# The last stage of an encoder-and-experts kernel: a buffer for every tile, the expert sum on TensorE, and two small outputs stored as rows

## What is computed

```python
# hier_moe: each row t has two experts with weights wts[t, 0:2]
out = out + comb[:, e:e + 1] * (hid @ w_expert_down[e])      # two rows of the sum per token are non-zero
x = x + gt2 * hier_moe(h)                                    # gated residual
y = rmsnorm(x, normf_g) * (1 + scf) + shf                    # final norm, scale and shift: outputs 0 and 1
# outputs 2 and 5: the last projected RWKV row of prompt and sample, 1664 numbers each
```

## Time and profile before

| | us |
|---|---|
| median of 3 runs (lowest, highest) | 1783.12 (1774.79, 1783.71) |
| the profiled execution | 1775.52 |
| its span, first to last instruction | 1773.8 |
| its first instruction of the last block | 1656.95 |

### The profile page before, as it was taken

One profiled execution on the slowest core, in us unless ns is written; L12 is line 12 of the kernel. 1 busy time (PEld: TensorE's weight loads), 2 busy tenths in 40 slices (PEclk: granted clock), 3 DMA queues, 4 the chain that ended last, 5 costly groups with the idle time before them and its releaser, 6 DMA issues. The chain is left out here.

```text
span 1773.8 us, 29923 instructions
## 1 busy us (share of the span) xinstructions
PE 1503.5 (85%) x12585; PEld 1096.1 (62%) x12585; DVE 547.6 (31%) x1006; ACT 384.8 (22%) x774; POOL 184.4 (10%) x281
## 2 busy tenths in 40 slices
PE   5899999999939999999999984699999999995100
PEld 3566665666628778776877652678878788683000
DVE  4254464302115545454545324110000000000066
ACT  5332223112113323332332220011111111100022
POOL 0011111100022001110111000100000000000031
PEclk9899999999969999999999966699999999997655
DMA  7345654422163321332132005997777877948563
GB/s 297 112 142 192 224 210 162 150 74 74 50 216 115 96 62 38 96 97 61 38 96 67 1 30 201 398 342 260 284 287 257 309 262 261 321 160 299 83 203 128
DMA packets 184095, 299.54 MB, mean 169 GB/s; under 512 B 22519, under 2 KB 94491, under 8 KB 183965
## 3 DMA queue, kind: packets, MB, share of 16 engines
q1 hardware_dynamic: 166860, 240.96, 39.7%
q0 software_dynamic: 12928, 42.79, 6.9%
q10 hardware_dynamic: 4176, 13.90, 2.0%
HBM read 241.96 MB, written 55.64 MB: 168 GB/s over the span
## 5 line engine op out<-in xcount | busy, mean ns | idle before, releaser
L2048 PE MATMUL banks<-moe_xT,moe_wg 128*128 128x160 f32 x1024 | 146.0, 301 | 0.8 <-ACT moe_xT L2168 0.8
L2048 PEld LDWEIGHTS banks<-moe_xT,moe_wg 128*128 128x128 f32 x1024 | 140.3, 190 | 7.6 <-issue 6.6
L2048 PE MATMUL banks<-moe_xT,moe_wu 128*128 128x160 f32 x1024 | 144.3, 299 | 0.0
L2048 PEld LDWEIGHTS banks<-moe_xT,moe_wu 128*128 128x128 f32 x1024 | 140.8, 190 | 0.0
L1215 PE MATMUL banks<-mixer_w_out,mixer_yT 128*128 128x512 f32 (+1 forms) x288 | 127.5, 601 | 4.5 <-DVE mixer_yT L1661 3.7
L598 PE MATMUL banks<-xT,w_v 128*128 128x352 f32 (+1 forms) x384 | 118.7, 469 | 0.0
L598 PE MATMUL banks<-xT,w_r 128*128 128x352 f32 (+1 forms) x384 | 118.6, 469 | 0.0
L598 PE MATMUL banks<-xT,w_k 128*128 128x352 f32 (+1 forms) x384 | 118.3, 468 | 0.0
L1471 POOL TENSOR_TENSOR mixer_LTm<-mixer_LT,level 128x256 f32<-128x256 f32 (+1 forms) x90 | 72.1, 825 | 407.3 <-ACT mixer_LTo L1527 282.3
L2089 PE MATMUL banks<-moe_wd,moe_hid 128*128 128x512 f32 x256 | 112.5, 592 | 0.0
L598 PEld LDWEIGHTS banks<-xT,w_v 128*128 128x128 f32 x384 | 72.6, 190 | 45.2 <-issue 2.2
(11 more groups left out here) (431 smaller groups left out, 2042.5 us busy)
## 6 DMA issues: line engine op xcount, KB each, us to landing
moe_wg<-w_expert_gate SPq DMA_DIRECT2D x20, 2048.0 KB, 9.2
moe_wu<-w_expert_up SPq DMA_DIRECT2D x20, 2048.0 KB, 11.8
moe_wd<-w_expert_down SPq DMA_DIRECT2D x20, 2048.0 KB, 10.0
w_mod<-w_ada SPq DMA_DIRECT2D x8, 2048.0 KB
mixer_feats<-feature_major SPq DMA_DIRECT2D x16, 768.0 KB, 8.4
wada<-w_ada SPq DMA_DIRECT2D x4, 2048.0 KB, 19.9
w_mod<-w_ada_final SPq DMA_DIRECT2D x4, 2048.0 KB
mixer_feats<-feature_major SPq DMA_DIRECT2D x8, 1024.0 KB, 5.8
```

What stands on the lines that cost most here:

```text
L2048: mm = pe.matmul(bank[:, i * S_STATIC:(i + 1) * S_STATIC], wt[:, u, q, (t0 + i) * P:(t0 + i + 1) * P], xT[:, e % 2, q, :], start=q == 0, s ...
```

## The change

- All 9 tiles have their own `y1`, `y2` and `x`; `x2` is written over `x`, the output over `y1`. The waits for a free buffer go. `idx` goes too: the gathers take their row numbers from `c["slots"]`. GpSimd issues all 18 gathers one behind the other without a wait; SyncE loads the first three `x` tiles at once and tile n when the gathers of tile n - 3 have landed.
- ScalarE makes, once, two diagonal matrices per tile (`diag`), the identity times each token's weight. TensorE multiplies `diag` by `y1` and `y2` and sums both products in PSUM, 4 matmuls of 128x128 by 512 columns per tile, into one of four pairs of banks. `first_share` and L2520 go; the gate product reads PSUM.
- TensorE turns the two small outputs to 13 rows of 128 numbers, ScalarE copies them to SBUF, and SyncE stores 512 B pieces, behind all its `x` loads.
- The squares go into `y2`. ScalarE issues the store of tile n - 1 after the exponential of tile n. VectorE's order of heads and tails is the same.

```diff
             experts_block(nc, a, d, c, psum, final_rows)
-            combine_block(nc, a, o, d, c, final_rows)
+            combine_block(nc, a, o, d, c, final_rows, banks)
...
-        y1, y2, x, x2, out = [sb(n, [P, 2, D]) for n in ("y1", "y2", "x", "x2", "out")]
-        idx = sb("idx", [P, 2, 2], I32)
-        st = sb("st", [P, 2, 2])
+        y1, y2, x = [sb(n, [P, NT, D]) for n in ("y1", "y2", "x")]
+        diag = sb("diag", [P, NT, 2, P])
+        st = sb("st", [P, NT, 2])
         eps = sb("eps", [P, 1])
-        slots, share = c["slots"], c["share"]
+        shifts_T = sb("shifts_T", [13, 2, P])
+        slots, share, ident = c["slots"], c["share"], c["ident"]
         GATE, SCALE, SHIFT = 0, 1, 2
         yp = o[0].rearrange("a t d -> (a t) d")
...
+        TILES = [(n, P if n < NP else DEC) for n in range(NT)]
+        def pair(n):
+            return banks[:, 1024 * (n % 4):1024 * (n % 4) + 1024]
...
         @block.sync
         def _(sp):
+            for n, m in TILES:
+                if n > 2:
+                    sp.wait_ge(sg(f"y{n - 3}_loaded"), 32)
+                sp.dma_start(x[0:m, n, :], d["x1"][n * P:n * P + m, :]).then_inc(sg(f"x{n}_loaded"), 16)
+            sp.wait_ge(sg("shifts_read"), 1)
             for r, i in ((0, 2), (1, 5)):
-                with nc.allow_non_contiguous_dma("a row of 13 x 128 from its columns"):
-                    sp.dma_start(o[i].rearrange("a b (n p) -> p (a b n)", p=P), c["shifts"][:, :, r]).then_inc(sg("shifts_out"), 16)
-            def step(n, u, m, n0, n1):
-                before = reg(sp, n - 1)
-                w(sp, "x2_made", before)
-                sp.dma_start(x[0:m, u, :], d["x1"][bass.ds(n * P, m), :]).then_inc(sg(f"x{u}_loaded"), 16)
-            tiles(sp, step)
+                sp.dma_start(o[i].rearrange("a b (n p) -> (a b n) p", p=P), shifts_T[:, r, :]).then_inc(sg("shifts_out"), 16)
             sp.wait_ge(sg("shifts_out"), 32)
         @block.gpsimd
         def _(pool):
             nc.gpsimd.memset(eps[:, :], RMS_EPS).then_inc(sg("eps_made"), 1)
-            def step(n, u, m, n0, n1):
-                before = reg(pool, n - 1)
-                w(pool, "x2_made", before)
-                nc.gpsimd.tensor_copy(idx[:, u, :], slots[:, bass.ds(n, 1), :].rearrange("p a b -> p (a b)")).then_inc(sg("idx_made"), 1)
+            for n, m in TILES:
                 for i, y in enumerate((y1, y2)):
-                    pool.wait_ge(sg("eps_made"), 1)
-                    pool.wait_ge(sg("idx_made"), n1)
-                    pool.indirect_dma_start(out=y[0:m, u, :], out_offset=None, in_=d["y"],
-                                            in_offset=bass.IndirectOffsetOnAxis(ap=idx[0:m, u, i:i + 1], axis=0)).then_inc(sg(f"y{u}_loaded"), 16)
-            tiles(pool, step)
+                    pool.indirect_dma_start(out=y[0:m, n, :], out_offset=None, in_=d["y"],
+                                            in_offset=bass.IndirectOffsetOnAxis(ap=slots[0:m, n, i:i + 1], axis=0)).then_inc(sg(f"y{n}_loaded"), 16)
+        @block.tensor
+        def _(pe):
+            for r in range(2):
+                mm = pe.transpose(banks[0:13, 7 * 512 + r * P:7 * 512 + (r + 1) * P], c["shifts"][:, :, r], ident[:, :])
+            mm.then_inc(sg("shifts_turned"), 1)
+            for n, m in TILES:
+                pe.wait_ge(sg("diag_made"), 2 * n + 2)
+                pe.wait_ge(sg(f"y{n}_loaded"), 32)
+                w(pe, "y_gated", n - 3)
+                if n == 3:
+                    pe.wait_ge(sg("shifts_read"), 1)
+                for h in range(2):
+                    for i, y in enumerate((y1, y2)):
+                        mm = pe.matmul(pair(n)[0:m, 512 * h:512 * h + 512], diag[0:m, n, i, 0:m], y[0:m, n, 512 * h:512 * h + 512],
+                                       start=i == 0, stop=i == 1)
+                mm.then_inc(sg("y_summed"), 1)
         @block.scalar
         def _(act):
             nc.scalar.preload_act_table_set("natural_log_exp_and_others")
+            act.wait_ge(sg("shifts_turned"), 1)
+            nc.scalar.copy(shifts_T[:, :, :], banks[0:13, 7 * 512:7 * 512 + 2 * P].rearrange("p (r c) -> p r c", r=2)).then_inc(sg("shifts_read"), 1)
+            for n, m in TILES:
+                for i in range(2):
+                    nc.scalar.activation(diag[:, n, i, :], ident[:, :], ACT.Copy, scale=share[:, n, i:i + 1]).then_inc(sg("diag_made"), 1)
             act.wait_ge(sg("eps_made"), 1)
-            def first_share(n, u, m):
-                act.wait_ge(sg(f"y{u}_loaded"), 16 * (n + 2 - u))
-                nc.scalar.activation(y1[0:m, u, :], y1[0:m, u, :], ACT.Copy, scale=share[0:m, n, 0:1]).then_inc(sg("y1_shared"), 1)
-            def step(n, u, m, n0, n1):
-                before = reg(act, n - 1)
-                if n == 0:
-                    first_share(0, 0, P)
-                w(act, "out_scaled", before)
-                w(act, f"out{u}_stored", 8 * (n - u))
-                w(act, "x2_made", n1)
-                nc.scalar.activation(out[0:m, u, :], x2[0:m, u, :], ACT.Square, accum_out=st[0:m, u, 0:1]).then_inc(sg("squared"), 1)
-                w(act, "squared", n1)
-                nc.scalar.activation(st[0:m, u, 1:2], st[0:m, u, 0:1], ACT.Ln, scale=1.0 / D, bias=eps[0:m, :]).then_inc(sg("log_made"), 1)
-                w(act, "log_made", n1)
-                nc.scalar.activation(st[0:m, u, 1:2], st[0:m, u, 1:2], ACT.Exp, scale=-0.5).then_inc(sg("rstd_made"), 1)
-                if n < NP:
-                    first_share(n + 1, 1 - u, DEC if n + 1 == NP else P)
-                act.wait_ge(sg("out_made"), n1)
-                dst = yp[bass.ds(n * P, m), :] if m == P else ys
-                act.dma_start(dst, out[0:m, u, :]).then_inc(sg(f"out{u}_stored"), 16)
-            tiles(act, step)
-            act.wait_ge(sg("out0_stored"), 80)
-            act.wait_ge(sg("out1_stored"), 64)
+            for n, m in TILES:
+                act.wait_ge(sg("x2_made"), n + 1)
+                nc.scalar.activation(y2[0:m, n, :], x[0:m, n, :], ACT.Square, accum_out=st[0:m, n, 0:1]).then_inc(sg("squared"), 1)
+                act.wait_ge(sg("squared"), n + 1)
+                nc.scalar.activation(st[0:m, n, 1:2], st[0:m, n, 0:1], ACT.Ln, scale=1.0 / D, bias=eps[0:m, :]).then_inc(sg("log_made"), 1)
+                act.wait_ge(sg("log_made"), n + 1)
+                nc.scalar.activation(st[0:m, n, 1:2], st[0:m, n, 1:2], ACT.Exp, scale=-0.5).then_inc(sg("rstd_made"), 1)
+                if n:
+                    act.wait_ge(sg("out_made"), n)
+                    act.dma_start(yp[(n - 1) * P:n * P, :], y1[:, n - 1, :]).then_inc(sg("out_stored"), 16)
+            act.wait_ge(sg("out_made"), NT)
+            act.dma_start(ys, y1[0:DEC, NP, :]).then_inc(sg("out_stored"), 16)
+            act.wait_ge(sg("out_stored"), 16 * NT)
...
-            def head(n, u, m, n0, n1):
+            def head(n, m):
                 r = 0 if m == P else 1
-                dve.wait_ge(sg(f"y{u}_loaded"), 16 * (n + 2 - u))
-                dve.wait_ge(sg("y1_shared"), n1)
-                V.scalar_tensor_tensor(y1[0:m, u, :], y2[0:m, u, :], share[0:m, n, 1:2], y1[0:m, u, :], ALU.mult, ALU.add).then_inc(sg("y_summed"), 1)
-                dve.wait_ge(sg("y_summed"), n1)
-                V.tensor_tensor(y1[0:m, u, :], y1[0:m, u, :], rows[0:m, r, GATE, :], ALU.mult).then_inc(sg("y_gated"), 1)
-                dve.wait_ge(sg(f"x{u}_loaded"), 8 * (n + 2 - u))
-                dve.wait_ge(sg("y_gated"), n1)
-                V.tensor_tensor(x2[0:m, u, :], x[0:m, u, :], y1[0:m, u, :], ALU.add).then_inc(sg("x2_made"), 1)
-            def tail(n, u, m, n0, n1):
+                dve.wait_ge(sg("y_summed"), n + 1)
+                V.tensor_tensor(y1[0:m, n, :], pair(n)[0:m, :], rows[0:m, r, GATE, :], ALU.mult).then_inc(sg("y_gated"), 1)
+                dve.wait_ge(sg(f"x{n}_loaded"), 16)
+                dve.wait_ge(sg("y_gated"), n + 1)
+                V.tensor_tensor(x[0:m, n, :], x[0:m, n, :], y1[0:m, n, :], ALU.add).then_inc(sg("x2_made"), 1)
+            def tail(n, m):
                 r = 0 if m == P else 1
-                dve.wait_ge(sg("rstd_made"), n1)
-                w(dve, f"out{u}_stored", 8 * (n - u))
-                V.scalar_tensor_tensor(out[0:m, u, :], x2[0:m, u, :], st[0:m, u, 1:2], rows[0:m, r, SCALE, :], ALU.mult, ALU.mult).then_inc(sg("out_scaled"), 1)
-                dve.wait_ge(sg("out_scaled"), n1)
-                V.tensor_tensor(out[0:m, u, :], out[0:m, u, :], rows[0:m, r, SHIFT, :], ALU.add).then_inc(sg("out_made"), 1)
-            def step(n, u, m, n0, n1):
-                head(n, u, m, n0, n1)
-                if not (isinstance(n, int) and n == 0):
-                    tail(n - 1, 1 - u, P, None, n0)
-            tiles(dve, step)
-            tail(NP, 0, DEC, NP, NT)
+                dve.wait_ge(sg("rstd_made"), n + 1)
```

(25 more changed lines are left out.)

## The result

The changed kernel takes 1726.7 us (median of 4 runs, 1722.7 to 1731.5) against 1783.1 for the kernel before (4 runs, 1774.8 to 1783.7): a ratio of 0.970, 95% interval 0.967 to 0.973. The forecast was 1725, range 1714 to 1744. The profiled execution took 1728.5 us, its span is 1726.1.

A forecast was written before the change was run, and what follows sets the result against it. Last block bound by a 23.69 us wait for first gathers and a ScalarE-VectorE ring of 9.67 us a tile; tile 1 summed 1674.0, plus 39.4, 2.5, 3.9: span 1719.8, plus 1.7 profiled, 3.5 run spread: 1725, range 1714 to 1744.

The forecast's parts named there:

- The single numbers: Two small outputs stored ahead of the last block's first gathers; removing them was to land tile 0 18.4 us earlier.
- The ring: Last block: ScalarE and VectorE take turns, 9.67 us a tile; breaking it was to save 39.5 us between first and last x2.
- The round: VectorE's four remaining operations per tile in the last block, start to start: 4.92 us.
- tail(8): VectorE's scale and shift for the last tile, after the 8 rounds: 2.5 us.
- the end: Issue and landing of the last store after VectorE's last operation: 3.9 us, unchanged.
- head(1): VectorE's gate product and residual of tile 1, starting at 1674.0; 8 rounds, 39.4 us, follow.
- The landing of tile 0: First tile's gathers in the last block, landed at 1664.6, with 6.0 us for the second gather; bounds 1662.1 and 1665.6.
- TensorE's start: First two tiles' sums: clock rises after 4.5 us of dense work, tile 0's sum at 1670.5, tile 1's at 1674.0.
- The clock didn't stay low: Rival: TensorE's clock stays low in the last block, 6.9 us a tile, span ends at 1738.2; chance 0.10.
- DMA wasn't the bound: Rival: DMA at 250 GB/s bounds the last block, end at 1739.3; chance 0.12, and 2 to 20 us.
- The small stores were the cause: Rival denied this: first gather slow by itself, tile 0 lands at 1683, span ends at 1738; chance 0.05.
- the slower case: Rival: busy VectorE keeps GpSimd from writing gather descriptors; slower than before from 10.4 us per gather on; chance 0.01.

The follow-up runs named there:

- rows-only: Kernel before with only the small outputs turned on TensorE and stored as 13 rows of 512 B behind all x loads: 1766.1 us against 1782.7, block 99.5 us.
- the second execution: The changed kernel profiled once more, unaltered, in the rounds of the kernel with both block-shortening steps: block 64.7 us, median 1727.7 us.

## Why the prediction was right, and where it was off

**The two causes.** Both were named before, and each was taken away alone. The single numbers cost 17.4 us in the old kernel and 17.3 in the new. I had 18.4 for the earlier landing of tile 0; the changed kernel gained 16.2 of it, and 17.5 when it ran again. The ring cost the rest: 99.5 to 65.5 us, 34.0 between the rows-only and the changed kernel, of which the buffers, the gathers and the new order of ScalarE's work make 29.1 together and TensorE's sum 4.9.

**The round** of 4.92 us, with a gate product on PSUM of 1219 ns against the 1225 worked out, came as foretold, and so did the 8 rounds (39.35 us against 39.4), tail(8) and the end. From head(1) on the two executions of the changed kernel both took 45.82 us to the end of the span.

**The landing of tile 0** is the term that was mis-sized: 9.86 us after the beginning, not 7.65, and 8.57 in the second execution, just inside my upper bound of 8.65. I took the 6.0 us of the earlier trace rows, where one `x` tile and one store lay beside a pair, though three `x` tiles are issued at once in the changed kernel; with them the piece measured 6.60 to 7.89 us in five kernels and executions. The first gather also began 0.73 us after the block, not 0.40: the first one has 0.63 us of issue in front of it, not 0.30.

**TensorE's start** was 0.4 us short, and 0.9 in the second execution: the clock rose after 5.1 and 6.1 us and not after 4.5.

**The rivals.** The clock didn't stay low, and pauses of 1.4 us didn't lower it. DMA wasn't the bound: tiles land every 3.75 us at 406 to 424 GB/s while VectorE takes 4.92. The margin was thinner than the forecast had it, for it rounded the sizes down: four times 128 rows of 4 KB are 2.10 MB, not 2, and in 4.92 us that is 426 GB/s, not 407, more than the 419 seen; a pair with its `x` tile is 1.57 MB, which in 6.0 us is 262 GB/s, not 250. What saved it is the other half of its argument: the loads run ahead of the stores. The small stores were the cause. GpSimd wrote its last four gathers beside a busy VectorE with issues of 1.51, 0.94, 1.85 and 0.89 us, far from the 10.4 that the slower case needed; nothing waited for them, and VectorE's operations kept their length. The 8 us that I had put on VectorE waiting for the gathers' issues didn't come; why such an issue doesn't hold VectorE up, as GpSimd's additions did, no run shows.

**The median.** That the sum met the median to 2 us is in part luck. For the profiled execution I had 1721.5 us and it took 1728.5: its block began 3.65 us later than that of before and was 2.65 longer than summed. The 3.5 us put on top for the spread of the runs happened to lie on that side, and the median of the runs lies 1.7 below the profiled one.

## What to carry to other kernels

Look at the packets' sizes before the first wait of a stage: two stores of 6.5 KB, number by number, cost 17 us, in which the engines would have moved 7 MB at the rate seen right behind them, issued ahead of the gathers that everything waited for. A ring of two engines was broken here by letting one run ahead (a buffer for each tile, the small product taken two tiles early, the store issued a tile later); moving an operation to an idle engine helped only behind that, and without it made this block 3.6 us longer. When an engine becomes the bound, count its operations in the trace, add them start to start: here that gave the period, 4.92 us, to a few hundredths.

## What the runs showed of the hardware

- Code that no experiment touches reached the last block anywhere between 1656.7 and 1668.8 us, later the more time TensorE had worked at the low clock. Comparisons of 3 us in this kernel need the stage's own length, not the program's time.
- TensorE's clock rose 3.8, 5.1 and 6.1 us after the dense work of the last block began, the last two in two executions of one kernel.
- The clock stayed at 2.4 GHz through pauses of 1.4 us between bursts of 3.67 us, and was at 1.2 GHz again each time TensorE came back after 7 to 11 us.
- A VectorE operation with two SBUF operands that starts beside a GpSimd addition took 2.28 us for 1.23; one with an operand in PSUM, begun 0.17 us before the addition, kept its 1.22. GpSimd's addition of 128x1024 took 2.35 us, less than the 3 that I had drawn from its 824 ns for 256 columns.
- The DMA engines gave 406 to 424 GB/s from 1668 to 1692 us with gathers, loads and stores mixed, while a gather took 10.9 us to land, the median over 1660 to 1692 us, against 6.0 in the earlier trace rows.
